# Handing the mixer's output to the output projection in SBUF instead of through DRAM

## The reference

```python
mixed = jnp.fft.fft2(ug, axes=(1, 3), norm="ortho").real      # u: 4 groups of 128 columns
y_fourier = jnp.einsum("blgc,gcd->blgd", mixed, w_fnet).reshape(bsz, seq, FNET_WIDTH)
...
y_rec = (rms_norm(o_fwd + o_bwd, out_norm) * gate)            # 4 heads of 128 columns
return jnp.concatenate([y_fourier, y_rec], axis=-1) @ w_out
...
x = x + hybrid_mixer(...)
h = rms_norm(x, norm_ffn)
affinity = softmax(h @ w_router); g, idx = top_k(affinity.T, cap)
```

## Time and profile before

| | us |
|---|---|
| three runs | 2831.88, 2836.04, 2839.47 |
| median | 2836.04 |
| profiled execution, its own time | 2837.88 |
| its span, first to last instruction | 2836.1 |
| mean granted TensorE clock | 0.977 |
| TensorE (PE) busy | 2679.7 (94%) |
| VectorE, ScalarE, GpSimd busy | 1659.1, 1346.9, 228.3 |
| DMA traffic | 515.87 MB, mean 182 GB/s |

### The profile page before, as it was taken

One profiled execution on the slowest core, in us unless ns is written; L12 is line 12 of the kernel. 1 busy time (PEld: TensorE's weight loads), 2 busy tenths in 40 slices (PEclk: granted clock), 3 DMA queues, 4 the chain that ended last, 5 costly groups with the idle time before them and its releaser, 6 DMA issues.

```text
span 2836.1 us, 33546 instructions
## 1 busy us (share of the span) xinstructions
PE 2679.7 (94%) x12878; PEld 2245.5 (79%) x12878; DVE 1659.1 (58%) x1996; ACT 1346.9 (47%) x1453; POOL 228.3 (8%) x255
## 2 busy tenths in 40 slices
PE   5999999998899479999999999999999999999997
PEld 4888888887687368888888888888888888888886
DVE  4454555543133766666666666666666666666666
ACT  5233333322243345555555555555555555465555
POOL 2010110100101120000000000000000000000010
PEclk9999999998999689999999999999999999999999
DMA  4000000103742356675766766667666666676666
GB/s 145 15 19 30 19 30 19 36 29 140 261 141 104 139 222 226 230 251 218 251 233 233 255 218 240 237 233 245 239 230 243 223 243 238 228 255 235 234 230 256
DMA packets 67477, 515.87 MB, mean 182 GB/s; under 512 B 7984, under 2 KB 8624, under 8 KB 42832
## 3 DMA queue, kind: packets, MB, share of 16 engines
q1 hardware_dynamic: 49680, 455.70, 43.9%
q0 software_dynamic: 17728, 59.24, 7.0%
HBM read 474.35 MB, written 40.89 MB: 182 GB/s over the span
## 4 chain that ended last, share of the span: by engine, by line
PE 63%; DVE 1%; DMA 0%; issue 0%; POOL 0%; ACT 0%; DVEq 0%; POOLq 0%
PE s_bank L1680 12%; PE s_bank L1679 12%; PE p_bank L1682 12%; PE s_bank L1681 12%; PE p_bank L1683 12%; PE etb L1659 1%; PE etb L1660 1%; DVE ew_raw L1515 0%; DMA xp<-ffn_in,next_token 0%; DVE where L941 0%; DVE table L942 0%; DVE best L940 0%; DVE x_parts L1555 0%; DVE table L1536 0%; DVE low L953 0%
## 5 line engine op out<-in xcount | busy, mean ns | idle before, releaser
L1548 DVE TENSOR_TENSOR big_lo<-ew_raw,big_hi 128x4096 fp32r<-128x4096 f32 x191 | 845.1, 4425 | 398.7 <-ACT big_hi L1393 398.7
L1393 ACT CAST big_hi<-ew_raw 128x4096 fp32r<-128x4096 f32 x192 | 698.3, 3637 | 71.9 <-PE p_bank L1683 58.1
L1679 PE MATMUL s_bank<-big_hi,x_parts 128*128 128x512 f32 x1024 | 402.8, 393 | 1.4 <-DVE x_parts L1557 1.4
L1680 PE MATMUL s_bank<-big_hi,x_parts 128*128 128x512 f32 x1024 | 398.9, 390 | 0.0
L1682 PE MATMUL p_bank<-big_hi,x_parts 128*128 128x512 f32 x1024 | 398.8, 389 | 0.0
L1681 PE MATMUL s_bank<-big_lo,x_parts 128*128 128x512 f32 x1024 | 398.7, 389 | 0.0
L1683 PE MATMUL p_bank<-big_lo,x_parts 128*128 128x512 f32 x1024 | 398.6, 389 | 0.0
L61 PE MATMUL bank<-big_hi,w_hi 128*128 128x512 f32 x576 | 237.8, 413 | 6.6 <-DMA lb<-in_lb_params 6.4
L63 PE MATMUL bank<-big_hi,w_lo 128*128 128x512 f32 x576 | 228.3, 396 | 0.0
L62 PE MATMUL bank<-big_lo,w_hi 128*128 128x512 f32 x576 | 227.7, 395 | 0.0
L1682 PEld LDWEIGHTS p_bank<-big_hi,x_parts 128*128 128x128 f32 x1024 | 192.2, 188 | 40.6
(11 more groups left out here) (248 smaller groups left out, 3779.7 us busy)
## 6 DMA issues: line engine op xcount, KB each, us to landing
ew_raw<-in_expert_weights SPq DMA_DIRECT2D x192, 2048.0 KB, 7.8
w_raw<-in_w_heads SPq DMA_DIRECT2D x48, 256.0 KB, 2.9
tab<-in_tables POOLq DMA_DIRECT2D x20, 512.0 KB, 5.4
x_in<-in_x SPq DMA_DIRECT2D x12, 512.0 KB, 4.1
raw_d<-mixer_y SPq DMA_DIRECT2D x24, 256.0 KB, 2.9
x_d<-in_x POOLq DMA_DIRECT2D x12, 512.0 KB, 4.8
residual<-x_d POOLq DMA_DIRECT2D x12, 512.0 KB, 2.9
ffn_in<-h_d POOLq DMA_DIRECT2D x12, 512.0 KB, 2.9
```

What stands on the lines that cost most here:

```text
L1393: nc.scalar.copy(w_hi[:, c % RING], raw[:, c % RAW]).then_inc(hi_done, 1)
L1548: nc.vector.tensor_tensor(w_lo[:, c % RING], raw[:, c % RAW], w_hi[:, c % RING].bitcast(F32), ALU.subtract).then_inc(lo_done, 1)
L1679: nc.tensor.matmul(s_bank[i][:], operand[:, t, S_HI], hi, start=a, stop=False)
L1680: nc.tensor.matmul(s_bank[i][:], operand[:, t, S_LO], hi, start=False, stop=False)
```

## The change

mixer_y keeps only the recurrence's half (4 x 128 x 1536). What each part does:

- In the Fourier stage the stores of y are gone, and with them the wait at the Block's end. SP instead loads, behind w_out's last split, the recurrence's 12 pieces (head_pieces) into wo_raw's space, seen as a ring of four. ScalarE casts them into big_hi and VectorE subtracts into big_lo at k 4 to 7, which P doesn't use.
- P's pieces are placed differently (p_piece): the prompt's in columns 0 to 511 of k 0 to 3, the sample's in columns 512 to 1535, where y of the same tokens belongs later.
- The first block's y is copied to f_out as before. When both sample blocks are complete, P of the sample isn't needed any more, and y is split in place: from f_out for the first block, from the banks for the second. The prompt's y is copied from the banks to f_out, two groups by ScalarE and two by VectorE, and the Block ends.
- In the output stage SP has no work. Neither has a product of the sample a split to wait for. f_out, which now lives through both stages (raw_d's space is gone), is split one group ahead of each of tiles 1 to 4.
- At the Fourier stage's start SP issues u's groups 2 and 3 only when group 0 has landed, and TensorE waits for m of two groups instead of four.

```diff
-        out = sb("f_out", [P, 4, BLK])
         banks = [ctx.enter_context(nc.psum_tensor(f"f_bank{i}", [P, BLK], F32)) for i in range(8)]
-        p_hi = hT_hi[:].rearrange("p k (a n) -> p (k a) n", n=BLK).rearrange("p (t g) n -> p t g n", g=2)
-        p_lo = hT_lo[:].rearrange("p k (a n) -> p (k a) n", n=BLK).rearrange("p (t g) n -> p t g n", g=2)
+        HR = 4
+        head_raw = wo_raw[:].rearrange("p a d -> p (a d)").rearrange("p (r n) -> p r n", n=BLK)
+        head_pieces = [(GROUPS + h, b) for b in (1, 2, 0) for h in range(HEADS)]
+        SAMPLE_AT = [(k, b) for k in range(GROUPS) for b in (1, 2)]
+        def at_piece(big, k, b):
+            return big[:, k, b * BLK:(b + 1) * BLK]
+        def p_piece(big, t, f):
+            first_sample = SEQS[0][1] // 2 // P
+            k, b = (2 * t + f, 0) if t < first_sample else SAMPLE_AT[2 * (t - first_sample) + f]
+            return at_piece(big, k, b)
...
+        head_loaded = [sem(f"head_loaded{i}") for i in range(HR)]
+        head_hi_done, head_lo_done = sem("head_hi_done"), sem("head_lo_done")
+        y_hi_done, y_lo_done, y_kept = sem("f_hi_done"), sem("f_lo_done"), sem("f_kept")
...
                 for g in range(GROUPS):
+                    if g == 2:
+                        sp.wait_ge(u_loaded[0], 16)
                     sp.dma_start(uT[:, g], u_dram[g]).then_inc(u_loaded[g], 16)
                 for k in range(KT):
                     if k >= 2:
                         sp.wait_ge(wo_lo_done, k - 1)
                     sp.dma_start(wo_raw[:, k % 2], w_out[k * P:(k + 1) * P]).then_inc(wo_loaded[k % 2], 16)
-                for i, (b, _, _) in enumerate(out_blocks):
-                    for g in range(GROUPS):
-                        sp.wait_ge(y_read, GROUPS * i + g + 1)
-                        sp.dma_start(y_dram[g, :, b * BLK:(b + 1) * BLK], out[:, g]).then_inc(y_stored[g], 16)
-                for g in range(GROUPS):
-                    sp.wait_ge(y_stored[g], 16 * NB)
+                sp.wait_ge(wo_lo_done, KT)
+                for n, (k, b) in enumerate(head_pieces):
+                    if n >= HR:
+                        sp.wait_ge(head_lo_done, n - HR + 1)
+                    sp.dma_start(head_raw[:, n % HR], y_dram[k - GROUPS, :, b * BLK:(b + 1) * BLK])\
+                        .then_inc(head_loaded[n % HR], 16)
...
-                for i in range(NB):
-                    for g in range(GROUPS):
-                        act.wait_ge(y_filled, GROUPS * i + g + 1)
-                        if i >= 1:
-                            act.wait_ge(y_stored[g], 16 * i)
-                        nc.scalar.copy(out[:, g], banks[4 * (i % 2) + g][:]).then_inc(y_read, 1)
+                for g in range(GROUPS):
+                    act.wait_ge(y_filled, g + 1)
+                    nc.scalar.copy(out[:, g], banks[g][:]).then_inc(y_read, 1)
+                for n, (k, b) in enumerate(head_pieces):
+                    act.wait_ge(head_loaded[n % HR], 16 * (n // HR + 1))
+                    nc.scalar.copy(at_piece(hT_hi, k, b), head_raw[:, n % HR]).then_inc(head_hi_done, 1)
+                act.wait_ge(y_filled, 2 * GROUPS)
+                for g in range(GROUPS):
+                    nc.scalar.copy(at_piece(hT_hi, g, 1), out[:, g]).then_inc(y_hi_done, 1)
+                    nc.scalar.copy(at_piece(hT_hi, g, 2), banks[4 + g][:]).then_inc(y_hi_done, 1)
+                act.wait_ge(y_filled, 3 * GROUPS)
+                act.wait_ge(y_lo_done, 2 * GROUPS)
+                for g in range(GROUPS // 2):
+                    nc.scalar.copy(out[:, g], banks[g][:]).then_inc(y_kept, 1)
...
+                for n, (k, b) in enumerate(head_pieces):
+                    dve.wait_ge(head_hi_done, n + 1)
+                    nc.vector.tensor_tensor(at_piece(hT_lo, k, b), head_raw[:, n % HR], at_piece(hT_hi, k, b).bitcast(F32),
+                                            ALU.subtract).then_inc(head_lo_done, 1)
+                for g in range(GROUPS):
+                    for b, y in ((1, out[:, g]), (2, banks[4 + g][:])):
+                        dve.wait_ge(y_hi_done, 2 * g + b)
+                        nc.vector.tensor_tensor(at_piece(hT_lo, g, b), y, at_piece(hT_hi, g, b).bitcast(F32),
+                                                ALU.subtract).then_inc(y_lo_done, 1)
+                dve.wait_ge(y_filled, 3 * GROUPS)
+                dve.wait_ge(y_lo_done, 2 * GROUPS)
+                for g in range(GROUPS // 2, GROUPS):
+                    nc.vector.tensor_copy(out[:, g], banks[g][:]).then_inc(y_kept, 1)
...
-                pe.wait_ge(m_ready, GROUPS)
                 for f in range(2):
+                    pe.wait_ge(m_ready, 2 * f + 2)
...
-                                ph, pl = p_hi[:, t0 + t, g // 2, at], p_lo[:, t0 + t, g // 2, at]
+                                ph, pl = (p_piece(big, t0 + t, g // 2)[:, at] for big in (hT_hi, hT_lo))
...
-        RR = 4
-        raw = sb("raw_d", [P, RR, BLK])
...
-        pieces = [(k, t // CH) for t in ORDER[::CH] for k in range(KT)]
...
-        later_pieces = lambda t: range(min(KT + 3 * t, len(pieces)), min(KT + 3 * t + 3, len(pieces)))
...
-            @block.sync
-            def _(sp):
-                for n, p in enumerate(pieces):
-                    if n >= RR:
-                        sp.wait_ge(lo_done, n - RR + 1)
-                    k, b = p
-                    sp.dma_start(raw[:, n % RR], y_dram[k, :, b * BLK:(b + 1) * BLK]).then_inc(raw_loaded[n % RR], 16)
...
-                def split(numbers):
-                    for n in numbers:
-                        act.wait_ge(raw_loaded[n % RR], 16 * (n // RR + 1))
-                        nc.scalar.copy(big_hi[xcols(*pieces[n])], raw[:, n % RR]).then_inc(hi_done, 1)
-
-                split(range(KT))
                 act.wait_ge(set_up, 7)
                 for t in range(TT):
-                    split(later_pieces(t))
+                    if 1 <= t <= GROUPS:
+                        nc.scalar.copy(big_hi[:, t - 1, prompt], f_out[:, t - 1]).then_inc(hi_done, 1)
...
-                def split(numbers):
-                    for n in numbers:
-                        at = xcols(*pieces[n])
-                        dve.wait_ge(hi_done, n + 1)
-                        nc.vector.tensor_tensor(big_lo[at], raw[:, n % RR], big_hi[at].bitcast(F32), ALU.subtract)\
-                            .then_inc(lo_done, 1)
-
-                split(range(KT))
                 dve.wait_ge(set_up, 7)
                 dve.wait_ge(const_loaded, 48)
                 for t in range(TT):
-                    split(later_pieces(t))
+                    if 1 <= t <= GROUPS:
+                        dve.wait_ge(hi_done, t)
+                        nc.vector.tensor_tensor(big_lo[:, t - 1, prompt], f_out[:, t - 1], big_hi[:, t - 1, prompt].bitcast(F32),
+                                                ALU.subtract).then_inc(lo_done, 1)
...
-                    b = t // CH
                     row = ORDER[t] * P
                     n = 2 * t + f
                     if n >= 4 and tiles[0] == 0:
                         pe.wait_ge(added, n - 3)
                     for k in tiles:
-                        if t % CH == 0 and f == 0:
-                            pe.wait_ge(lo_done, b * KT + k + 1)
+                        if t == S_TILES and f == 0 and k < GROUPS:
+                            pe.wait_ge(lo_done, k + 1)
...
-    y_dram = nc.dram_tensor("mixer_y", (KT, P, NT), F32, kind="Internal").ap()
+    y_dram = nc.dram_tensor("mixer_y", (HEADS, P, NT), F32, kind="Internal").ap()
...
-        with nc.sbuf_tensor("wo_hi", [P, KT, D], F32R) as wo_hi, nc.sbuf_tensor("wo_lo", [P, KT, D], F32R) as wo_lo:
+        with (nc.sbuf_tensor("wo_hi", [P, KT, D], F32R) as wo_hi, nc.sbuf_tensor("wo_lo", [P, KT, D], F32R) as wo_lo,
+              nc.sbuf_tensor("f_out", [P, GROUPS, BLK], F32) as f_out):
             fourier_phase(nc, u_dram, w_fnet, channel_dft, tables, w_out, big_hi, big_lo, u_space, wo_hi,
-                          wo_lo, y_dram)
-            output_phase(nc, x, norm_ffn, w_router, identity, y_dram, acc, h_dram, routing, big_hi, big_lo, wo_hi, wo_lo)
+                          wo_lo, y_dram, f_out)
```

15 lines of the change are left out of this document (7 added, 8 removed).

## The result

The changed kernel took 2819.72 us (median of 4 runs, 2816.13 to 2825.66), the kernel before beside it 2834.93 (4 runs): a ratio of 0.995, 95% interval 0.9938 to 0.9962, or 15.2 us. The forecast was 2820.7. Run again later beside three others it took 2820.05 against 2834.15, ratio 0.9948 (0.9935 to 0.9962), 14.1 us.

The account below looks back on a forecast made before the run. TensorE's chain, 63% of the span, was taken as the bound: 13.8 (first tile) - 0.7 (clock) + 2.2 (splits) = 15.3 us off 2837.88 gives 2822.6, as median 2820.7 us; range 2814 to 2829.

Parts of the forecast that it names:

- the prediction's own signs: Wrong if the Fourier stage grows, TensorE stands between 760 and 785, or the gain is missing at the experts' first product.
- One sign failed: Expected in the changed kernel's profile: transposes 13.6 us apart in all tiles without selection.
- if the first tile gained only half of 13.8: Rival at the output stage's start: the wait is only replaced by the next late thing, w_router or x; 2828.5 us, 5%.
- Part 1: End of the Fourier stage: 12 stores and their landing wait go, first output product at 760.5, bounds 760.0 to 761.0.
- Part 2: First output tile: full pace without split waits, ending 771.4 against 785.2, 13.8 us gained, less 0.7 for a slow clock.
- Part 3: Recurrence's pieces loaded and split during the Fourier products: 2.1 us of cover, cost 0, bounds 0 and +3.
- pieces late: Rival: the recurrence's pieces outlast their 2.1 us of cover in the Fourier stage, +1.8 to +3, 2823.5 us; 13%.
- Part 4: Table loads beside the pieces in the Fourier products: 2.4 us of cover, cost zero; 5.6 us if tables take 8.3.
- the prediction's 9.4 us: Time a table would take in the Fourier products if it queued behind all four pieces, losing 14 us in sum.
- Part 5: Splits between the output tiles: one instead of three in tiles 1 to 4, 2.2 us gained, ends 1.2 and 2.8.
- Part 6: Fourier stage's start, u's groups 2 and 3 issued after group 0 lands: 0 taken, gain 0 to 1.9, no loss.

Follow-up runs that it names:

- e2_u_wait_only: Kernel before with only the change's start: the wait for u's group 0, and TensorE waiting for m of two groups; 2832.57 us, one run.
- e11_after_warm: Changed kernel plus 18 products nobody reads while TensorE stands for the first expert's rows; 2819.64 us, ratio 0.9944.
- e1: Changed kernel without its wait ahead of u's group 2; 2817.61 us, ratio 0.9933 to the kernel before.
- e5: e1 with the recurrence's first two pieces issued one w_out split earlier; 2819.31 us, ratio 0.9939 to the kernel before.
- e6: e5 plus 18 products nobody reads while TensorE stands for the first expert's rows; 2815.26 us, ratio 0.9932 to the kernel before.
- e12: The kernel of e6 run again, beside the changed kernel; 2819.32 us, ratio 0.9945 to the kernel before.

## Why the prediction was right

The sum was 15.3 us; by the trace 15.14 in the first execution. From u's issue to tile 5's transposes the kernel before took 189.43 us (189.37 in e2_u_wait_only, where a start that is 1.06 us longer and a first tile that is 1.08 us shorter cancel), the changed one 174.29, 173.86 in its repeat and 175.80 in e11_after_warm: 14.8 us less on average, and 15.2 and 14.1 in the two comparisons of times. Behind tile 5 nothing systematic was gained or lost. That the profiled pair gained 12.2 us and the medians 15.2 shows how much of so close an agreement is luck.

By the prediction's own signs, the Fourier stage didn't grow (55.66 to 55.76 us in all profiles), TensorE didn't stand inside the first tile, and 16.5 us had been gained at the experts' first product. One sign failed: the transposes are 13.6 us apart in all tiles without selection but the fourth (14.08; 14.41 before). One of its sums is off: if the first tile gained only half of 13.8, 8.4 of the 15.3 us are left and not 7.5. Nothing hung on that rival.

*Part 1* said 1.9 us of stop and was sized right: 1.64 or 1.65 in all six profiles in which the stores are gone and the pieces on time, with copies of 1.29 us in it. It read the old stop as a landing, a change of stage and a load with its splits. Of these the landing was tested by itself: one store put back costs 2.26 us.

*Part 2* said 10.9 us for the tile, 10.98 by the starts of its first product and of tile 1's. It took half of 1.4 us for a slow start of the clock; behind a stop of 1.65 us the clock stayed at 1.00 in six of six profiles, so nothing was due. Behind 2.09 and 3.26 us it stayed too, behind 2.95, 5.34 and 8.94 it fell and cost 1.5 to 1.8 us, so the end of 1.4 was a little low. w_router landed 4.5 us after its issue. x landed at 773.0, 4 us after TensorE's first half tile (768.9), VectorE's first addition waited for it until 773.2, and TensorE didn't have to.

*Part 3* had the right chain and, in three profiles of five, the right end (a cover of 2.1 us said, 1.6, 2.4 and 3.2 measured), and the wrong kind of uncertainty. It set "pieces late" as a rival of 13% that is true of the kernel or not. It is true of an execution: twice in five, for 1.4 to 1.5 us of stop. The terms behind it: pieces landed after 4.9 us (median of 12; 5.2 taken), but the first issue came 25.9 to 29.4 us after the first Fourier product where the prediction had 26.2, as w_out's loads, too, end at different times. The expected cost was not 0 but about 0.6 us.

*Part 4* was right. The tables behind the loads of pieces, and the pieces, us from issue to landing, stretch 734 to 750 of after:

```profile
wo_raw<-mixer_y SPq DMA_DIRECT2D x12, 256.0 KB, 4.9
tab<-in_tables POOLq DMA_DIRECT2D x6, 512.0 KB, 5.0
```

A table took 5.0 us there (5.2 in the earlier trace rows), and TensorE stood for none, in this or any other profile. The Trainium skill (DMA: Bandwidth & Descriptors, Queues, rings and completion order) says that each DMA engine takes turns between the queues that have work. This agrees with it: a table behind all four pieces would have taken the prediction's 9.4 us.

*Part 5*: 2.2 us said, 2.44 measured, 2.71 when the splits were put back. Tile by tile it is 0.64, 0.72, 0.67, 0.33 and 0.08 us: in the fourth tile half of what the others lose was there too, where the sum counted 0.1 for the last two.

*Part 6* failed. It gave the wait ahead of u's group 2 "0, gain 0 to 1.9", and no loss, because VectorE takes up group 2 only behind the other two. The step that was wrong is that no number was put on how late group 2 comes: it is issued when group 0 has landed, takes as long as that did (6.8 us from u's issue to the first fold), and so lands 7.1 us after it, at 690.73, while two groups of folds last only 5 us (683.66 to 688.6). VectorE stood 1.1 to 2.2 us in all eight profiles with the wait. How much of it reaches TensorE depends on when the clock rises in this stage: about 1.4 us where it rises early (1.22 in the first pair of profiles), 0.1 where it rises late, 0.7 on average. What makes it rise early or late isn't known.

So a loss of 0.1 to 1.4 us that was missed and one of 0 to 1.5 that was set at zero lie against 0.7 us taken for the clock and 0.2 of splits. The total was close to the forecast partly because these cancel.

Whether a version beats the changed kernel stays open. Without the u wait the comparison gives 18.5 us (e1), with early pieces 18.1 (e5), with all three edits 22 once (e6) and 14.8 once (e12), against 15.2 and 14.1 for the changed kernel. The traces allow some 0.7 us for the wait, and 0.6 for pieces that would never be late, which the early issue isn't shown to achieve; the runs of one kernel scatter by 2 to 10.

## What to carry to other kernels

A result that goes through DRAM between two stages costs more than its transfers: the landing of the last store, the change of stage, the first load and its split stood in line, 7.3 us of TensorE's time, and a second round of the ring and a slow clock behind them cost 7 to 8 more. Work moved into the shadow of another stage is free as long as its chain ends first. With a cover of 2 us and a chain of 12 loads whose end moves by nearly 5 us between executions, count that it does not in some of them, and read the margin in several profiles. A load that waits for another's landing comes a full landing time after it: compare that with the work that covers it, instruction by instruction. And before a difference of 1 us between two profiles is put down to an edit, look when the clock rose in each: at this stage's start that alone moved the mark by about 1 us.
